# Convolution norm inside the input projection, pooling means on GpSimd, head norms and mixed tiles woven into the output projection's first block

## The reference, cut to what matters

```python
h  = modulate(rms_norm(x, norm1_g), sh1, sc1)
q, k, v, u_pool, a_conv, b_conv = split(h @ w_in)         # q, k: rms norm per 64, axial rope
a  = softmax(q0 k0) - lam * softmax(q1 k1)                # 4 heads, differential attention
attn = rms_norm(a @ v, subln_g) * (1 - lambda_init)       # per head of 128: the "head norm"
p  = window_sum(u_pool, w) / count - u_pool               # w = 2, 4, 8, 16: the "means"
pool_o = (p @ pool_w) * pool_scale                        # 64 x 64 per group
y  = depthwise_conv31(a_conv * sigmoid(b_conv)) + dw_b    # 256 channels
conv_o = silu(layer_norm(y, ln_g, ln_b))                  # over the 256 channels: the "convolution norm"
x = x + g1 * (concat([attn, pool_o, conv_o]) @ w_out)     # 1024 x 1024
x = x + g2 * swiglu(modulate(rms_norm(x, norm2_g), sh2, sc2))
```

## Time and profile before

| | |
|---|---|
| three runs | 2661.23, 2663.3, 2669.94 us; median 2663.3 |
| profiled execution | 2661.66 us, span 2659.8 us |
| busy share of the span | PE 94%, DVE 49%, ACT 30%, POOL 32% |
| mean granted TensorE clock | 0.953 |
| layer 0: last value product of attention ends, output block 1 starts | 370.53 us, 420.55 us |
| layer 1: the same, end of output block 0 | 1302.12 us, 1335.00 us |

### The profile page before, as it was taken

The page is one execution under the profiler, slowest core; times in us unless marked ns, Lnnn a source line. Parts: engine busy times, 40 slices in busy tenths (PEclk is TensorE's granted clock), DMA queues, the critical chain, the costliest instruction groups (busy, mean ns, idle before and its releaser), DMA issues.

```text
span 2659.8 us, 30852 instructions
## 1 busy us (share of the span) xinstructions
PE 2509.1 (94%) x13105; PEld 2054.2 (77%) x13105; DVE 1314.4 (49%) x1692; ACT 797.4 (30%) x1079; POOL 846.3 (32%) x601
## 2 busy tenths in 40 slices
PE   7999879999999999898899999989999989999998
PEld 4888768888888888697677778878887437788886
DVE  2994765645444344876556655564642323311113
ACT  2322652311111112335632122234343333322223
POOL 2001102233333233443034455544443002444442
PEclk9998889899999999898899999989999998999999
DMA  8232103224333332221034555531103001232331
GB/s 271 83 103 88 48 1 99 77 84 139 119 110 105 123 98 89 72 96 48 1 95 132 155 157 151 169 108 48 48 17 111 16 0 48 72 100 83 98 96 60
DMA packets 309226, 240.57 MB, mean 90 GB/s; under 512 B 10693, under 2 KB 304832, under 8 KB 309088
## 3 DMA queue, kind: packets, MB, share of 16 engines
q1 hardware_dynamic: 308674, 238.47, 29.6%
q10 hardware_dynamic: 414, 0.13, 0.0%
HBM read 232.29 MB, written 2.10 MB: 88 GB/s over the span
## 4 chain that ended last, share of the span: by engine, by line
PE 85%; DVE 9%; ACT 3%; issue 1%; DMA 1%; POOL 0%; SPq 0%; DVEq 0%; ACTq 0%
PE ps L2399 59%; PE ps L1106 5%; PE ps L2427 3%; PE ps L713 2%; PE ps L926 2%; PE ps L664 1%; DVE mod_w L2034 1%; PE ps L1126 1%; DVE mod_ctx L2034 1%; PE ps L888 1%; PE ps L1149 1%; DVE conv_acc L1033 1%; PE ps L740 1%; DVE small L1000 1%; PE ps L2305 1%
## 5 line engine op out<-in xcount | busy, mean ns | idle before, releaser
L1589 POOL TENSOR_TENSOR w_lo<-raw,w_hi 128x512 fp32r<-128x512 f32 x518 | 755.8, 1488 | 1633.7 <-ACT w_hi L1683 1633.7
L2399 PE MATMUL ps<-h_hi,w_hi 128*128 128x512 f32 x1994 | 646.3, 370 | 34.8 <-DVE h_lo L1998 21.9
L2399 PE MATMUL ps<-h_lo,w_hi 128*128 128x512 f32 x1994 | 641.5, 368 | 0.0
L2399 PE MATMUL ps<-h_hi,w_lo 128*128 128x512 f32 x1994 | 640.5, 367 | 0.0
L1683 ACT ACTIVATE w_hi<-raw 128x2048 fp32r<-128x2048 f32 (+2 forms) x155 | 264.8, 1708 | 649.0 <-PE ps L2399 373.5
L2399 PEld LDWEIGHTS ps<-h_hi,w_hi 128*128 128x128 f32 x1994 | 341.7, 191 | 106.6 <-issue 31.3
L2399 PEld LDWEIGHTS ps<-h_hi,w_lo 128*128 128x128 f32 x1994 | 341.1, 191 | 67.5
L2399 PEld LDWEIGHTS ps<-h_lo,w_hi 128*128 128x128 f32 x1994 | 341.3, 191 | 66.6
L1925 ACT ACTIVATE xg<-ps 128x512 f32<-128x512 f32 (+1 forms) x66 | 44.2, 670 | 678.1 <-PE ps L2399 491.3
L2034 DVE SCALAR_TENSOR_TENSOR mod_w<-mod_w,cond 128x512 f32<-128x512 f32 x217 | 233.5, 1076 | 3.4
L2399 PE MATMUL ps<-hid_hi,w_hi 128*128 128x512 f32 x704 | 231.4, 369 | 0.0
(11 more groups left out here) (364 smaller groups left out, 3245.8 us busy)
## 6 DMA issues: line engine op xcount, KB each, us to landing
mod_w<-in_w_mod SPq DMA_DIRECT2D x72, 1024.0 KB, 9.7
raw<-in_w_ffn_in SPq DMA_DIRECT2D x88, 512.0 KB, 5.3
raw<-in_w_in SPq DMA_DIRECT2D x54, 512.0 KB, 5.0
raw<-in_w_ffn_out SPq DMA_DIRECT2D x48, 384.0 KB, 3.8
raw<-in_w_out SPq DMA_DIRECT2D x24, 512.0 KB, 4.5
raw<-in_w_gate SPq DMA_DIRECT2D x22, 512.0 KB, 4.0
raw<-in_w_up SPq DMA_DIRECT2D x22, 512.0 KB, 5.4
raw<-in_w_down SPq DMA_DIRECT2D x24, 384.0 KB, 3.9
```

Of the source, the lines that this page charges most:

```text
L1589: ins = pool.tensor_tensor(w_lo[:, s, at:end], raw[:, s, at:end], w_hi[:, s, at:end].bitcast(F32), ALU.subtract)
L2399: ins = pe.matmul(ps[0:m, at:at + tw], weight(part, k, cols), v[:, k, t0:t0 + tw], start=(at_k == 0 and j == 0 and not shared), stop=(at_k ...
```

## The change

- **Convolution norm.** The sums over channels (`conv_sums`) run on PE after tile 0 of block 7, DVE centres right after its rotations of q, ACT squares after block 6, PE sums the squares after block 7 (`conv_square_sums`) ahead of `head_sums(2)`, and the root is turned in block 8 (`conv_root_turned`). DVE scales after its rotations of k, ACT does Silu into `conv_acc` itself at the end of its part of block 7. `own_lo(8)` moves behind pair (0, 6). Turning the first root of k waits for the scaled convolution (`c_yn`).
- **Pooling means.** POOL multiplies and subtracts right after the window edges; `window_means` is gone from DVE's attention, and `pool_ready` with it.
- **Head norms.** The sums of squares of heads 0 to 2 and the pooling product of tile 4 (and the context piece of tile 5) run on PE inside the last unit, before its turn. The root of heads 0 to 2 follows at once; head 3 is summed after the first k-step of output block 0, and the roots are turned after k-steps 1, 2 and 3.
- **Mixed tiles.** The k order becomes convolution, pooling, heads. `MIX_AT` gives each mixed tile another place in `h_hi` and `h_lo`, so that the convolution's and the pooling's are written before the last probabilities are done with.

```diff
-        MIX_ORDER = [4, 5, 0, 1, 2, 3, 6, 7]
-        SUM_AT, SUM_C = 3072, 3584
+        MIX_ORDER = [6, 7, 4, 5, 0, 1, 2, 3]
+        MIX_AT = [4, 5, 6, 7, 2, 3, 0, 1]
+        SUM_AT, SUM_LAST, CONV_AT, SUM_C = 3072, 3584, 3072, 3072 + 128
...
@@ attention: PE, ACT
+                if u == len(us) - 1:
+                    before_last()
                 turn(u)
...
+                if u == len(us) - 1:
+                    before_last()
                 copy_turned(u)
...
+            before_save()
             save(len(us) - 1)
...
@@ POOL
-                    pool.engine_nop().then_inc(pool_ready, 1)
+                    for win, rows in ((win_s, slice(0, 64)), (win_t, slice(64, 128))):
+                        for t0, tw in parts[l]:
+                            at = POOL_CTX if t0 else POOL_LAT
+                            inner, u = win[rows, :, at:at + tw], u_pool[rows, :, at:at + tw]
+                            share = const[rows, C_INVI:C_INVI + 2].unsqueeze(2).to_broadcast([64, 2, tw])
+                            link(pool.tensor_tensor(inner, inner, share, ALU.mult))
+                            ins = pool.tensor_tensor(u, inner, u, ALU.subtract)
+                    ins.then_inc(pooled, 1)
...
@@ ACT, input projection
+                        if b == 6:
+                            for t in range(2):
+                                act.wait_ge(c_yc, 2 * l + t + 1)
+                                for t0, tw in parts[l]:
+                                    at = t0 + (PAD if t0 else 0)
+                                    ins = act.activation(c_square[:, t, t0:t0 + tw], conv_acc[:, t, at:at + tw], ACT.Square)
+                                ins.then_inc(c_sq, 1)
                         if b == 7:
+                            act.wait_ge(c_ss, l + 1)
+                            act.activation(c_root, ps[:, SUM_C:SUM_C + tiles], ACT.Sqrt, bias=eps, scale=1.0 / 256
+                                           ).then_inc(c_std, 1)
+                            act.wait_ge(c_inv, l + 1)
+                            spread(act, c_square[:, 0, 0:T], c_root, tiles).then_inc(c_spread, 1)
                             roots(3)
                             spread_root(4)
                             spread_root(5)
+                            for t in range(2):
+                                act.wait_ge(c_yn, 2 * l + t + 1)
...
+                                    ins = act.activation(y, y, ACT.Silu, bias=..., scale=...)
+                                ins.then_inc(c_f, 1)
...
@@ ACT, last unit and tail
+                    def conv_hi():
+                        act.wait_ge(pooled, l + 1)
+                        for t in range(2):
+                            for t0, tw in parts[l]:
+                                act.wait_ge(c_f, 2 * l + t + 1)
+                                ins = act.activation(h_hi[:, MIX_AT[6 + t], t0:t0 + tw], conv_acc[:, t, at:at + tw], ACT.Copy)
+                            ins.then_inc(m_hi, 1)
...
+                    def before_save():
+                        root_of_heads(0, HEADS - 1, 1)
+                        pool_hi(0)
+
                     double_act(act, l, lambda u: qk[:, u["h"], u["g0"]:u["g0"] + u["gw"]], head_square,
-                               None if l else attention_pair)
+                               None if l else attention_pair, conv_hi, before_save)
+                    pool_hi(1)
+                    act.wait_ge(m_inv, 2 * l + 1)
+                    for h in range(HEADS - 1):
+                        spread_head(h)
+                    root_of_heads(HEADS - 1, HEADS, 2)
+                    act.wait_ge(m_inv, 2 * l + 2)
+                    spread_head(HEADS - 1)
...
@@ DVE, input projection
+                    dve.wait_ge(c_sum, l + 1)
+                    for t in range(2):
+                        for t0, tw in parts[l]:
+                            ins = dve.scalar_tensor_tensor(y, ps[:, CONV_AT + t0:CONV_AT + t0 + tw], -1.0 / 256, y,
+                                                           ALU.mult, ALU.add)
+                        ins.then_inc(c_yc, 1)
                     if l == 0:
+                        pair_all((0, 6))
                         own_lo(8)
-                        pair_all((0, 6))
                         own_lo(9)
                     for j in range(2, 4):
                         inverse(j)
                         rotate(j)
+                        if j == 2:
+                            dve.wait_ge(c_std, l + 1)
+                            dve.reciprocal(c_root, c_root).then_inc(c_inv, 1)
+                    dve.wait_ge(c_turned, l + 1)
+                    for t in range(2):
+                        for t0, tw in parts[l]:
+                            ins = dve.tensor_tensor(y, y, ps[:, CONV_AT + t0:CONV_AT + t0 + tw], ALU.mult)
+                        ins.then_inc(c_yn, 1)
...
-                        if u == len(units[l]) // 2:
-                            window_means()
...
@@ PE, input projection
+                            if b == 7:
+                                conv_square_sums()
                             if b >= 5:
                                 head_sums(b - 5)
                         else:
-                            between = {1: lambda: head_sums(3)} if b == 8 else {
+                            between = {1: lambda: head_sums(3), 3: conv_root_turned} if b == 8 else {
...
@@ PE, last unit and output block 0
+                    def before_last_unit():
+                        pe.wait_ge(at_exp, last_exp - 2)
+                        for h in range(HEADS - 1):
+                            ins = head_square_sums(h, tiles * h)
+                        ins.then_inc(m_ss, 1)
+                        pe.wait_ge(pw_in, 64 * (l + 1))
+                        pe.wait_ge(pooled, l + 1)
+                        pe.wait_ge(at_exp, last_exp)
                         for t0, tw in parts[l]:
+                            ins = pool_product(0, t0, tw)
+                        ins.then_inc(pw_ps, 1)
+                        if len(parts[l]) == 2:
+                            pool_product(1, *parts[l][1])
+
+                    double_pe(pe, l, lambda kt, h: v_nat[:, kt, h * P:h * P + P], None if l else attention_pair,
+                              before_last_unit)
+                    pool_product(1, *parts[l][0]).then_inc(pw_ps, 1)
+                    pe.wait_ge(m_arg, 2 * l + 1)
+
+                    def last_head_sums():
+                        pe.wait_ge(at_saved, pv_base[l + 1])
+                        head_square_sums(HEADS - 1, SUM_LAST).then_inc(m_ss, 1)
...
+                    def turn_heads(*heads):
+                        for h in heads:
+                            pe.wait_ge(m_spread, 4 * l + h + 1)
+                            if h < 2:
+                                pe.wait_ge(m_lo, 8 * l + 4)
+                                pe.wait_ge(m_arg, 2 * l + 2)
+                            else:
+                                pe.wait_ge(m_o, 4 * l + h - 1)
+                            turn_wide(pe, 2048 + 1024 * (h % 2), qk[:, 4 + h, :], tiles).then_inc(m_turned, 1)
+
+                    mix_between = {0: last_head_sums, 1: lambda: turn_heads(0, 1), 2: lambda: turn_heads(2),
+                                   3: lambda: turn_heads(3)}
```

More of the change, by code:

```diff
@@ L1883, in _ @@
-                    act.wait_ge(m_arg, l + 1)
-                    act.activation(n_root[:, 0:HEADS * tiles], n_root[:, 0:HEADS * tiles], ACT.Sqrt, scale=1.0 / P
-                                   ).then_inc(m_std, 1)
-                    for t in range(2):
-                        act.wait_ge(c_yc, 2 * l + t + 1)
-                        for t0, tw in parts[l]:
-                            at = t0 + (PAD if t0 else 0)
-                            ins = act.activation(c_square[:, t, t0:t0 + tw], conv_acc[:, t, at:at + tw], ACT.Square)
-                        ins.then_inc(c_sq, 1)
@@ new lines, in root_of_heads, with spread_head @@
+                    def root_of_heads(first, end, number):
+                        act.wait_ge(m_arg, 2 * l + number)
+                        root = n_root[:, tiles * first:tiles * end]
+                        act.activation(root, root, ACT.Sqrt, scale=1.0 / P).then_inc(m_std, 1)
+                    def spread_head(h):
+                        spread(act, qk[:, 4 + h, 0:T], n_root[:, tiles * h:tiles * (h + 1)], tiles).then_inc(m_spread, 1)
+                    def before_save():
+                        root_of_heads(0, HEADS - 1, 1)
+                        pool_hi(0)
@@ L2377, in views, with products @@
                 return [t[:, s, 0:k * w].rearrange("p (k n) -> p k n", n=w) for t in (w_hi, w_lo)]
-            def products(n, k_tiles, width, sp_, hi, lo, k_ready=None, then=None, order=None, place_at=None, ni=None):
+            def products(n, k_tiles, width, sp_, hi, lo, k_ready=None, then=None, order=None, place_at=None, ni=None,
+                         between=None, held=None):
```

(33 more changed lines are left out.)

202 lines of the change are left out of this document (83 added, 119 removed).

## The result

The changed kernel takes 2649.79 us (median of 5 runs, 2646.87 to 2653.95), the kernel before 2663.18 beside it (5 runs, 2661.23 to 2669.94): ratio 0.995, interval 0.9932 to 0.9968, so 13.4 us or 0.5% less. A second set of runs of the same kernel gave 2651.47 beside 2665.05 (0.9949, 0.9935 to 0.9964); the median of its eleven runs is again 2649.79. The forecast was 2653.2, and 10.1 us less than before. The profiled execution took 2653.95 and is the slowest of its five; its span is 7.6 us under that of before.

A forecast was written before the change was run, and what follows sets the result against it. PE work and PE's waits, partly at half clock, were taken to bound it. Terms: -8.8 - 13.4 + 10.6 + 6.1 - 3.1 - 1.5 = -10.1, giving 2651.6, as median 2653.2 us; range 2641 to 2663.

The forecast's parts named there:

- Tail of layer 0: Attention's end to output block 1: block 1 starts 15.7 us sooner, less clock charges; net -8.8, bounds -15.7 and -6.
- replay: Layer 0's tail recomputed with the rows' durations: block 0 starts at 377.0, block 1 at 404.8 instead of 420.55.
- Tail of layer 1: Attention's end through output block 0, no pair to wait for: -14.9, less 1.5 for the clock; -13.4.
- Convolution norm, layer 0: Input projection around blocks 7 and 8: added PE work and a later pair, +10.6 us, bounds +6.5 and +12.
- Layer 1: Convolution norm in layer 1: sums and turn count in full, +4.1, plus 2.0 for the clock; +6.1.
- The means: Attention, both layers: DVE loses 7.6 us of pooling work, contention with POOL costs 4.5; net -3.1.
- The norm: Norm after each tail: Sqrt stays loaded, so the table load on the chain goes; -1.5, bounds -1.5 and -2.6.
- B: Rival, whole kernel: the clock gives nothing back, so -25.7 with contention, 2637.5 us; chance 0.15.
- D: Rival, tails: narrow sums hold PE at 0.50 through all of output block 0; +31, 2684 us; chance 0.1.
- C: Rival: no measurable change; block 9 waits 3 us per layer on ACT, contention costs 7; 2661.7 us; chance 0.2.

The follow-up runs named there:

- version with the steps in the waits: Changed kernel with 11 of the 16 VectorE steps of output block 0's pair put into idle stretches of layer 0's tail: 2634.71 us.
- the single edit: Changed kernel with the pooling means back on VectorE, in the middle unit of each attention: 2646.05 us.
- the sums behind the last unit: Changed kernel with the column sums of the first three heads moved from ahead of the last attention unit to behind it, both layers: 2651.61 us.
- the split of pair (0, 6): Changed kernel with 5 of the 16 VectorE steps of layer 0 block 7's pair put ahead of the wait for the convolution's sums: 2652.31 us.

## Why the prediction was right

Term by term the stages bear the sum out to within 2 us each in the first profile, except inside the term of the means, where a cost and a saving were both set too low and cancel. The closeness of the total is in part luck: 10.1 us were forecast, the medians give 13.4 and the two profiles 7.6, and executions of the changed kernel alone lie up to 13 us apart.

**Tail of layer 0**, forecast -8.8: from the first scores to block 1 it is -13.1 (143.3 us for 156.4), and with the 2.15 us that blocks 1 and 2 now pay (36.17 for 34.02) it is -11.0; with the means' share of about -0.3 in it, -10.7. The stall of 5 us before the pair's sums was there (5.3), the pair's sums (+1.9) and block 1 (+2.15) paid as forecast. Too dear were the 3.0 for half speed after the sums in the last unit: block 0's first product came at 386.67, 9.7 us after the replay's 377.0 in which attention starts at the old time; with the 8.9 of the input stage taken off, 0.8 is left for them (1.1 beside the 0.3 that the attention gained). The version with the steps in the waits bears the replay out: without the stall and the clock behind it, the prediction's replay gives -15.7 - 5 = -20.7, and that version has -10.7 - 9.3 = -20.0.

**Tail of layer 1**, forecast -13.4: -12.7 in the first profile, with the last value products at low clock, -15.5 in the second (22.5 us from the sums to the end of block 0, for 25.3).

**Convolution norm, layer 0**, forecast +10.6: +8.9. The pair's sums start 2.8 later (forecast 3.4) and take 1.6 more, the sums of squares are 5.1, the turn 0.66; the products and sums behind them took 1.3 less than before (41.9 us without the turn, for 43.2), since the clock had risen sooner. Doubling the sums of squares cost 5.4. So each row of 24 costs what it was charged, and half of that is the clock's: at full speed 24 of them cost 2.6. The lower bound of +6.5 does not follow from its own terms (10.6 less 1.2 and 3.8 is 5.6); by the rows, the 16 at full speed would give back 1.9 and the 24 another 2.5, hence +6.2.

**Layer 1**, forecast +6.1: +6.8 (144.4 us for 137.6, both in the first of the two forms described below). The sums and the turn are 3.8, and behind them the head sums take 4.11 for 2.57 and the first products of v 7.48 for 5.76.

**The means**, forecast -3.1: this is the term whose parts were mis-sized. Contention was charged 4.5 and measured 6.7, with GpSimd's instructions at 25.4 us in all where 18.4 were expected; the saving was set at 7.6 and measured 10.6, since VectorE's instructions cost layer 0's chain 7.3 us and not the 4.6 of their own durations: 2.0 of the rest is the low clock that follows TensorE's idle behind them. Both errors cancel in the changed kernel (-3.9 by the single edit). Compared with the kernel before, the attention of layer 0 is only 0.3 us shorter, and layer 1's up to the last unit 1.6 longer in the first profile and equal in the second (73.1 us for 73.0). In layer 0 2 us went to the attention pair's sums, of which all four groups now took 3.50 us where before the first two took 1.88 and 2.79; that is so with the means on VectorE too, so it is not the move's doing. Seven of the fourteen profiles have all four at 3.50, seven have the first at 1.88, and both forms occur with the means on GpSimd. In the kernel before the move alone brought nothing (0.9992). Of the difference between 3.9 and 0 the clock is 1.5: the value products behind VectorE's means took 3.31 in the kernel before (its chain, at 338.25) and 4.82 in the changed one. The rest stays open.

**The norm**, forecast -1.5: no load in either layer, -1.2 in each. In layer 0 it was worth more than the 0.2 set for it.

**The rivals.** B fell with the rows at 0.50, D with the clock at 1.00 through the whole of output block 0 (its first half, 386.6 to 399.1, as well). C's waits did not come: the turns of block 9 stand without a gap. The measured stages sum to -8.7, the spans differ by 7.6, and the other 1.1 us lie in stretches that the change does not touch.

**What stays open** is the rest of the medians. Some edits have leads over the changed kernel that their stages explain only in part (the means on VectorE, and the versions with the pair moved). The profiles show places where executions differ though the code is the same: the attention pair's sums in layer 0 and the length of layer 1's attention, both named above, and two that go together. Behind the wait of layer 1's block 1 for its weights' low part TensorE starts either at 0.50 or at 1.00, and in the versions with the new sums of squares the head sums 60 us later go the same way. In the changed kernel:

```profile
1111.73 25.19 PE ps L2454 x96
...
1177.79 4.11 PE ps L2537 x24
```

With the pair in the tail's waits:

```profile
1101.99 22.66 PE ps L2458 x96
...
1165.52 2.68 PE ps L2541 x24
```

Layer 1's input stage, where it has the changed kernel's code, is 144.3 us in the first form and 140.2 in the second. Of fourteen profiled executions eight have the first form, the kernel before and both of the changed kernel among them; five have the second (the means on VectorE, the sums behind the last unit, and three of the four versions with the pair of output block 0 moved), and the fourth of these lies between (24.20 and 3.83). None of these edits touches that stage. The time at which the block starts does not decide either: the version with the sums behind the last unit starts it at 1111.73 us like the changed kernel, and has the other form (granted clock 1.00 from 1111.7 to 1115.0, for 0.50). With one or two profiles of a kernel it can't be told whether an edit shifts the odds or the profiled execution drew it; that it is worth 4 us of a median was not shown.

## What to carry to other kernels

Work on a helper engine that stood hidden under a block becomes a stall when the block moves forward: list what each engine has queued behind the moved work, and cut that into the waits that the move leaves (here 9.3 us by stages, 15 by the medians, for three edited places). Rows of one- and two-column matmuls ran at either level here (24 in 2.57 to 5.12 us): where such a row stands behind idle or behind another such row, as in block 7, price it at twice its full-speed time as the upper bound; ahead of the last unit and between wide products it kept near full speed in the changed kernel (36 in 4.18, 12 in 1.23). Where one edit is worth under 0.3%, read it by stages and by more than one execution: medians of five or six runs gave the same edit opposite signs. Check, too, that a stage's gain is not there in a version without the edit, as the split of pair (0, 6) showed.

## What the runs showed of the hardware

- The clock fell to 0.50 within a row of 64 narrow products during which TensorE was never idle (16 in 1.68 us, 24 in 3.43, 24 in 5.12), and in one more execution within the same row behind 1.25 us of idle (1.92, 5.08, 5.12). In layer 1, behind 16 at full speed, 24 ran near full speed in five executions (2.68 us) and not in seven (3.83 to 5.12).
- After idle of 5.3 us the 16 sums of output block 0 took 3.57 for 1.68, and the two blocks after them lost 2.2 us more (36.17 for 34.02). In block 7 the same number of sums took 3.54 behind idle of 4.40 us and 1.92 behind 1.25.
- VectorE's instruction with two operands in SBUF (1.02 us alone) took 3.30 beside a GpSimd instruction of 2.8, and ended 0.8 us behind that one's end (1237.63 and 1236.81). GpSimd's eight long instructions in layer 0 and four in layer 1 (not 16 and 8, as one expectation says) lasted 15.1 and 10.3 us and cost the chain 6.7 us, about a quarter of their time. The Trainium skill, page "SBUF — State Buffer", section "SBUF: two separate sides", states that the two engines hold shared ports exclusively; the runs agree, but the outcome to which its rule alone pointed, that the move gains nothing, was measured only in the kernel before.
